# Norm roots moved to ScalarE, and a block of eight modulation units moved from TensorE to GpSimd, in a four-layer float32 transformer kernel

## The chip, the cores and the metric

The kernel runs on one core of a Trainium2 chip. The metric is the device time of one execution in microseconds (us); three executions of the kernel before took 2784.01, 2784.29 and 2785.72 us, median 2784.29.

## The reference

The program computes four transformer layers over 256 tokens of width 1024 in float32. The change touches the first layer's modulation and the norms.

```python
def rms_norm(x, gain=None):
    y = xf * lax.rsqrt(jnp.mean(xf * xf, axis=-1, keepdims=True) + EPS)
...
def _layer_norm(x, g, b):
    mu = jnp.mean(xf, -1, keepdims=True)
    var = jnp.mean(jnp.square(xf - mu), -1, keepdims=True)
    return ((xf - mu) * lax.rsqrt(var + LN_EPS) * g + b)
...
    c_act = jax.nn.silu(c)
    for l in range(DEPTH):
        mod = (c_act @ ada_w[l] + ada_b[l])[:, None, :]
        sh_m, sc_m, gt_m, sh_f, sc_f, gt_f = jnp.split(mod, 6, axis=-1)
        h = rms_norm(x, norm_mix[l]) * (1 + sc_m) + sh_m
        y = hybrid_mixer(h, ...) if l % 2 == 0 else retention_mixer(h, ...)
        x = x + gt_m * y
        h = rms_norm(x, norm_ffn[l]) * (1 + sc_f) + sh_f
        x = x + gt_f * swiglu(h, ffn_w_in[l], ffn_w_out[l])
```

The hybrid mixer has two halves: a gated delta rule (GDN) and a stick-breaking attention (stick). Two more layers follow, each with a mixer of a recurrence and attention, a layer norm (`l1`), a router over 128 groups of experts, and a second layer norm (`l2`).

## The kernel before, in words

**Weights.** All weights come as units of 128x1024 words through a ring of four buffers (`raws`, `NRAW = 4`), loaded by SyncE in the order of the list `units`. The load of unit j waits until unit j-4 has been used up. A unit for an ordinary product is halved: ScalarE rounds it to its high part (`wr<-raw`, 128x1024) and VectorE subtracts that for the low part (`wr<-raw,wr`); TensorE then makes three products of high and low parts. `split()` on both engines does this up to two units ahead of the unit that TensorE is at. A modulation unit (`modulate`, blocks of 512 columns of `ada_w`, four units each) isn't halved: TensorE multiplies it as it is with `cact`, four matmul records of 512 columns per unit. Blocks 7 and 9 (`ADDED`) are already summed by VectorE (`keep<-raw,small,keep`), and one product with a matrix of ones (`add_up`) adds them over the partitions.

**Order.** `order(s)` is one hand-written list of steps which each engine's program runs through. `bg.run(n)` weaves in n steps of background strands (the convolution, `gdn`, `stick`). In the first layer: the first modulation blocks (`FIRST`), twelve `qkv` units, four `gate_rows` units, then the `gdn` strand is added, then the eight units of `SECOND` (blocks 4 and 5) with 3 background steps between, then twelve `stick_rows` units with 3 background steps each (the `stick` strand joins after the eighth), then the sixteen units of `THIRD` with `add_up` of blocks 7 and 9, and the output product `hybrid_out`. The `gdn` strand begins with ScalarE's squares, four sums and their roots (`G.act root`), one chain of small VectorE instructions (`softplus`), transposes (`tok`), and then seven `levels` for two halves of the tokens.

**Norms.** `ada_norm` (before the two feed-forward products and the retention mixer) and `layer_norm` (`l1`, `l2`) have the same shape: squares or statistics for each half a of the tokens, a root per token, a diagonal matrix of the inverse roots (`mod_diag`, `ln_diag`), and TensorE's products with that diagonal, which transpose and scale at once. Before the change VectorE makes the variance (L2487 or L2287), ScalarE the square root, VectorE the reciprocal (L2492) and the diagonal (L2286). `norm_bias` halves the row of biases that TensorE adds with 16 matmuls (`sel,keep_r`).

```python
        def row_scale(tag, v, diag, a):
            dve.wait_ge(*N.act[tag, "root", a])
            dve.reciprocal(v, v).then_inc(*N.dve.up())
            own(N)
            ts(diag[a], ident, v, None, ALU.mult).then_inc(*N.dve.up((tag, "diag", a)))
```

**GpSimd** issues the small loads at the start and the later modulation loads (`aux`); its only arithmetic is in the later mixers (`kin`, L3476).

## Time and profile before

| | |
|---|---|
| median of three executions | 2784.29 us |
| the profiled execution | 2786.23 us |
| its span (first to last instruction) | 2784.4 us |
| TensorE busy | 2720.1 us (98%) |
| VectorE / ScalarE / GpSimd busy | 2206.1 (79%) / 1609.3 (58%) / 87.2 us (3%) |
| mean DMA rate | 208 GB/s |
| granted TensorE clock | 1.0 in the stretches read below |

The profile gives busy time per engine; a busy share near 100% on TensorE says that most of the time is product work, but not that each removed product shortens the run. For that the stretch around it is read: which engine's instruction did the next one wait for. In the lists of rows, PE is TensorE, PEld its weight loads, DVE is VectorE, ACT is ScalarE, POOL is GpSimd and SP is SyncE.

### The profile page before, as it was taken

Reading aid. Unit: us, or ns where it says so; the run is one execution under the profiler, and the core shown is the slowest. Engines: PE = TensorE matmul, PEld = TensorE weight load, DVE = VectorE, ACT = ScalarE, POOL = GpSimd, SP = SyncE. Lnnn points to the kernel's source line nnn. Section 1 sums busy time; section 2 is a strip of 40 time slices with the busy share of each in tenths; the row PEclk is TensorE's granted clock in tenths of the full one; section 3 lists DMA queues with packets and bytes.
Section 4 is the critical chain, followed back from the end, with each engine's and each line's share of the span. In section 5 each row is a group of like instructions: output and inputs, shape, how many; then the busy total and the mean of one; then the engine's idle time right before and its main releaser. Section 6 shows DMA issues by size and latency. Waiting matters only on the chain.

```text
span 2784.4 us, 45458 instructions
## 1 busy us (share of the span) xinstructions
PE 2720.1 (98%) x17102; PEld 2429.6 (87%) x17102; DVE 2206.1 (79%) x3874; ACT 1609.3 (58%) x2793; POOL 87.2 (3%) x154
## 2 busy tenths in 40 slices
PE   8998999999999999999999999999999999999998
PEld 5777888978888989999998888898999999988886
DVE  4766888886665678999887888876799988788887
ACT  3433654345554744778985555555457799754543
POOL 1000101010002000000000000020000000000000
PEclk9999999999999999999999999999999999999999
DMA  8433777764556335666558777762466665687774
GB/s 298 153 114 135 279 257 252 260 247 154 197 189 240 105 136 190 222 212 211 195 196 273 241 242 243 231 213 84 154 209 221 206 208 195 213 269 242 242 242 161
DMA packets 211289, 579.71 MB, mean 208 GB/s; under 512 B 24096, under 2 KB 87872, under 8 KB 210048
## 3 DMA queue, kind: packets, MB, share of 16 engines
q1 hardware_dynamic: 161568, 491.00, 53.2%
q0 software_dynamic: 13792, 53.28, 5.5%
q10 hardware_dynamic: 35712, 32.52, 3.4%
q8 instruction: 138, 2.26, 0.3%
q14 instruction: 79, 0.65, 0.1%
HBM read 541.05 MB, written 35.65 MB: 207 GB/s over the span
## 4 chain that ended last, share of the span: by engine, by line
PE 85%; DVE 9%; ACT 3%; issue 1%; DMA 1%; ACTq 0%; DVEq 0%; POOLq 0%
PE psum L779 84%; DVE gmem L2290 3%; DVE wr L2290 2%; ACT gmem L1636 1%; DVE gmem L2293 1%; ACT wr L1636 1%; DVE xmem L2293 1%; ACT crf L1636 1%; DMA raw<-in_hyb_qkv 0%; DVE wr L2293 0%; DVE small L3125 0%; DVE gmem L2286 0%; DVE gmem L3247 0%; DVE xmem L2290 0%; PE psum L894 0%
## 5 line engine op out<-in xcount | busy, mean ns | idle before, releaser
L779 PE MATMUL psum<-xr,wr 128*128 128x256 f32 (+1 forms) x9776 | 1284.7, 292 | 3.7 <-DVE wr L2290 3.7
L2290 DVE TENSOR_TENSOR wr<-raw,wr 128x1024 fp32r<-128x1024 f32 (+1 forms) x814 | 992.6, 1222 | 365.7 <-ACT wr L1636 361.1
L779 PEld LDWEIGHTS psum<-xr,wr 128*128 128x128 f32 x9776 | 1232.3, 192 | 38.5 <-issue 4.1
L1636 ACT ACTIVATE wr<-raw 128x1024 fp32r<-128x1024 f32 x808 | 845.2, 1050 | 220.9 <-PE psum L779 160.0
L779 PE MATMUL psum<-wr,cr 128*128 128x512 f32 x2064 | 483.0, 389 | 1.8 <-ACT cr L1636 1.8
L779 PEld LDWEIGHTS psum<-wr,cr 128*128 128x128 f32 x2064 | 387.5, 188 | 82.3 <-ACT cr L1636 2.2
L1636 ACT ACTIVATE gmem<-psum 128x512 f32<-128x512 f32 (+2 forms) x303 | 168.9, 570 | 200.4 <-PE psum L779 185.6
L779 PE MATMUL psum<-wr,keep_r 128*128 128x512 f32 x1008 | 243.3, 390 | 0.5 <-DVE wr L2290 0.5
L779 PE MATMUL psum<-wr,xr 128*128 128x512 f32 (+1 forms) x960 | 229.6, 392 | 4.7 <-DVE wr L2290 2.0
L779 PEld LDWEIGHTS psum<-wr,keep_r 128*128 128x128 f32 x1008 | 189.2, 188 | 40.4 <-DVE wr L2290 1.3
L2293 DVE SCALAR_TENSOR_TENSOR oh_r<-cst,keep,keep_r 128x256 fp32r<-128x256 f32 x512 | 213.2, 479 | 0.0
L779 PEld LDWEIGHTS psum<-wr,xr 128*128 128x128 f32 x960 | 172.4, 189 | 45.0 <-issue 6.5
L779 PE MATMUL psum<-gmem 128*128 128x128 f32 (+6 forms) x1320 | 188.5, 295 | 14.8 <-DVE gmem L2290 5.4
L779 PEld LDWEIGHTS psum<-gmem 128*128 128x128 f32 (+1 forms) x1320 | 169.4, 192 | 33.0 <-DVE gmem L2290 7.4
L1636 ACT ACTIVATE cr<-xmem 128x256 fp32r<-128x256 f32 x172 | 72.0, 418 | 215.3 <-PE psum L779 211.1
L1636 ACT ACTIVATE xmem<-psum 128x256 f32<-128x256 f32 x256 | 97.1, 379 | 163.2 <-PE psum L779 153.3
L2290 DVE TENSOR_TENSOR xmem<-xmem,gmem 128x256 f32<-128x256 f32 (+1 forms) x272 | 169.7, 625 | 0.6
L1636 ACT ACTIVATE crf<-cst,keep 128x128 f32<-128x128 f32 x512 | 162.7, 393 | 0.4
L2290 DVE TENSOR_TENSOR gmem<-gmem,psum 128x512 f32<-128x512 f32 x163 | 110.3, 682 | 40.4 <-PE psum L779 25.2
L779 PE MATMUL psum<-wr,hid_r 128*128 128x512 f32 x528 | 122.6, 393 | 0.0
L2290 DVE TENSOR_TENSOR gmem<-gmem 128x256 f32<-128x256 f32 (+10 forms) x195 | 114.0, 593 | 8.8 <-ACT gmem L1636 5.9
L779 PEld LDWEIGHTS psum<-wr,hid_r 128*128 128x128 f32 x528 | 98.9, 188 | 22.5 <-issue 1.9
(193 smaller groups left out, 1732.4 us busy)
## 6 DMA issues: line engine op xcount, KB each, us to landing
raw<-in_uv SPq DMA_DIRECT2D x512, 512.0 KB, 4.7
raw<-in_ffn_in SPq DMA_DIRECT2D x88, 512.0 KB, 4.2
gs<-xmem ACTq DMA_DIRECT2D x248, 128.0 KB, 3.7
xmem<-gs SPq DMA_DIRECT2D x248, 128.0 KB, 4.3
gmem<-in_ada_w POOLq DMA_DIRECT2D x56, 512.0 KB, 4.9
raw<-in_ffn_out SPq DMA_DIRECT2D x44, 512.0 KB, 4.1
raw<-in_ada_w SPq DMA_DIRECT2D x40, 512.0 KB, 4.3
raw<-in_ret_a SPq DMA_DIRECT2D x32, 512.0 KB, 4.3
```

What stands on the lines that cost most here:

```text
L779: ins = pe.matmul(o, a, b, start=first and i == 0, stop=final and i == len(pairs) - 1, skip_group_check=skip)
L1636: return act.activation(o, a, func, **k)
L2290: return dve.tensor_tensor(o, a, b, op)
L2293: return dve.scalar_tensor_tensor(out=o, in0=a, scalar=s, in1=b, op0=op0, op1=op1)
```

## The change

It does five things.

1. `SECOND` is no block of its own: its eight units stand in `units` between the first eight `stick_rows` units, one after each, and `stick_rows` has 5 background steps in place of 3.
2. TensorE no longer multiplies these units. GpSimd scales each half of a unit by its column of `cact` in place and adds it to a sum (`ada_acc`), 30 instructions of 128x512 words in all; a wait on its own semaphore stands between them. SyncE's load of four units later waits for GpSimd (`summed`). TensorE adds each of the two sums up with `add_up`, after the first and third unit of `THIRD`.
3. In `ada_norm` and `layer_norm` the variance, root, inverse and diagonal are made by ScalarE: a logarithm with scale and bias, an exponential with scale -0.5, and the identity scaled by it. VectorE's `row_var` and `row_scale` are gone. The preloaded table is the one with logarithm and exponential.
4. The norm `on` of the attention half (`nsa_turn`) takes the same inverse root.
5. `norm_bias` of `l1` moves from `mix_out` to `mix_col` 11, and the last norm's VectorE steps are reordered.

```diff
+    POOLED = (4, 5)
...
-    add_plain(SECOND)
-    units += [(dr["hyb_a"][c][i], UNIT) for c in range(1, 4) for i in range(4)]
+    pool_unit = {}
+    for r_ in range(12):
+        units.append((dr["hyb_a"][1 + r_ // 4][r_ % 4], UNIT))
+        if r_ < len(SECOND):
+            pool_unit[SECOND[r_]] = len(units)
+            add_plain(SECOND[r_:r_ + 1])
...
-        for i, (m, q) in enumerate(SECOND):
-            if i > 1:
-                bg.run(3)
-            s["modulate"](m, q)
...
                 s["stick_rows"](c, i)
-                bg.run(3)
+                bg.run(5)
+                if 4 * c + i < len(SECOND):
+                    s["modulate"](*SECOND[4 * c + i])
...
             s["modulate"](m, q)
+            if i in (0, 2):
+                s["add_up"](POOLED[i // 2])
...
+        def row_scale(tag, v, bias, scale, diag, a):
+
+            f(v, v, AF.Ln, scale=scale, bias=bias).then_inc(*N.act.up())
+            act.wait_ge(*N.act.now)
+            f(v, v, AF.Exp, scale=-0.5).then_inc(*N.act.up((tag, "root", a)))
+            if diag:
+                act.wait_ge(*N.act.now)
+                f(diag[a], ident, AF.Identity, scale=v).then_inc(*N.act.up((tag, "diag", a)))
...
                     f(used[:, a, e], x[:, a, e], AF.Square,
                       accum_out=small_v[:, i:i + 1]).then_inc(*N.act.up((tag, "sq", i)))
-                v = small_v[:, 4 + a:5 + a]
-                act.wait_ge(*N.dve[tag, "var", a])
-                f(v, v, AF.Sqrt, bias=epsc).then_inc(*N.act.up((tag, "root", a)))
+                    act.wait_ge(*N.act.now)
+                    if n == 0:
+                        f(part, small_v[:, i:i + 1], AF.Identity, scale=1.0 / D, bias=epsc).then_inc(*N.act.up())
+                row_scale(tag, small_v[:, 2 * a + 1:2 * a + 2], part, 1.0 / D, mod_diag, a)
...
-                act.preload_act_table(AF.Sqrt)
+                act.preload_act_table_set("natural_log_exp_and_others")
...
+            if i == 11:
+                act.wait_ge(ln1_in[l], 32)
+                norm_bias(("l1", l), l1b)
...
-                root(S, ("on", l), rn[:, 2:4])
+                inverse_root(S, ("on", l), rn[:, 2:4])
...
-                f(v, v, AF.Sqrt).then_inc(*N.act.up((tag, "root", a)))
+                row_scale(tag, small_v[:, 25 + 2 * a:26 + 2 * a], lneps, 1.0, ln_diag if split_ else None, a)
...
+        pool.wait_ge(*X.act["cact"])
+        for m, q in SECOND:
+            j, acc = pool_unit[m, q], ada_acc[m]
+            pool.wait_ge(raw_in[j % NRAW], 16 * (j // NRAW + 1))
+            for k in range(2):
+                r, c = raws[j % NRAW][:, k * 512:(k + 1) * 512], cact[:, 2 * q + k:2 * q + k + 1]
+                if q + k == 0:
+                    pool.tensor_scalar(acc, r, c, None, ALU.mult).then_inc(*summed.up())
+                else:
+                    pool.wait_ge(*summed.now)
+                    pool.tensor_scalar(r, r, c, None, ALU.mult).then_inc(*summed.up())
+                    pool.wait_ge(*summed.now)
+                    pool.tensor_tensor(acc, acc, r, ALU.add).then_inc(*summed.up(("used", j) if k else None))
```

TensorE's order where the GDN strand starts, before. Names: `wr,xr` is a halved weight unit, `raw,small` a modulation unit, `gmem,cst_60` the four sums of squares, L1025 the transposes.

```order
L779 MATMUL psum<-wr,xr 128x512 x12
L779 MATMUL psum<-raw,small 128x512 x4
L779 MATMUL psum<-gmem,cst_60 128x512 x2
L779 MATMUL psum<-raw,small 128x512 x2
L779 MATMUL psum<-gmem,cst_60 128x512 x2
L779 MATMUL psum<-gmem,cst_60 128x8 x2
L779 MATMUL psum<-raw,small 128x512 x2
L1025 MATMUL psum<-cst_60,gmem 128x128 x12
```

The same place now:

```order
L785 MATMUL psum<-wr,xr 128x512 x24
L785 MATMUL psum<-gmem,cst_60 128x512 x4
L785 MATMUL psum<-wr,xr 128x512 x12
L785 MATMUL psum<-gmem,cst_60 128x8 x2
L1031 MATMUL psum<-cst_60,gmem 128x128 x16
```

The modulation products are gone, and one stick unit stands before the four sums (the other 12 of the first row belong to the last gate unit) and one behind them. The transposes follow the second with no weight unit between them.

ScalarE's order at the same place, before: the gate's activation, the convolution's activation, the table for the sigmoid, the sigmoid, the next table, the squares of the GDN strand.

```order
L1636 ACTIVATE gmem<-psum 128x512 x2
L1636 ACTIVATE gmem<-gmem 128x1024
L1636 ACT_TABLE_LOAD
L1636 ACTIVATE gmem<-gmem 128x8
L1768 ACT_TABLE_LOAD
L1636 ACTIVATE gmem<-gmem 128x512 x4
```

And now:

```order
L1642 ACTIVATE gmem<-psum 128x512 x2
L1642 ACTIVATE gmem<-gmem 128x1024
L1642 ACTIVATE wr<-raw 128x1024
L1642 ACT_TABLE_LOAD
L1642 ACTIVATE gmem<-gmem 128x8
L1785 ACT_TABLE_LOAD
```

The high part of a stick unit now stands ahead of the sigmoid and of the squares.

ScalarE's order at the end of a later mixer, from the norm `on` (128x2) to the norm `l1` (128x1), before:

```order
L1636 ACT_TABLE_LOAD
L1636 ACTIVATE small<-small 128x2
L1636 ACTIVATE wr<-raw 128x1024
L1636 ACTIVATE keep_r<-oh 128x1024
L1636 ACTIVATE small<-small 128x1 x2
L1636 ACTIVATE xr<-psum 128x4x128 x4
```

And now:

```order
L1642 ACT_TABLE_LOAD
L1642 ACTIVATE small<-small 128x2
L1642 ACT_TABLE_LOAD
L1642 ACTIVATE small<-small 128x2
L1642 ACTIVATE wr<-raw 128x1024
L1642 ACT_TABLE_LOAD
L1642 ACTIVATE small<-small 128x1
L1642 ACT_TABLE_LOAD
L1642 ACTIVATE small<-small 128x1
L1642 ACTIVATE gmem<-cst_60,small 128x128
L1642 ACT_TABLE_LOAD
L1642 ACTIVATE small<-small 128x1
```

One more table load, the exponential and the diagonal of the second half follow: six table loads here in place of one, in each of the two later mixers. In the other norms the number of table loads is unchanged. The halving of the bias row (`keep_r<-oh`) has left this place.

## Rows read from the trace of the kernel before

**Rows 1.** The page: the chain that ended last, by engine.
```profile
PE 85%; DVE 9%; ACT 3%; issue 1%; DMA 1%; ACTq 0%; DVEq 0%; POOLq 0%
```

**Rows 2.** Busy time by stretch: the columns are named in the first line.
```profile
core 0: us, PE busy (x) PEld busy (x) DVE busy (x) ACT busy (x) POOL busy (x), PEclk, DMA share, GB/s
89.00:112.00 23.00, 20.55 (x85) 11.98 (x83) 12.84 (x40) 12.67 (x24) 0.00 (x0) 1.00 0.33 110
127.20:163.40 36.20, 35.38 (x210) 30.57 (x208) 25.09 (x33) 12.46 (x15) 0.00 (x0) 1.00 0.46 163
```

**Rows 3.** Timeline, TensorE: start, duration, engine, instruction, [idle before it <- releaser].
```profile
94.59 3.01 PE L779 MATMUL psum<-wr,xr 128*128 128x512 f32 x12
98.29 3.70 PE L779 MATMUL psum<-raw,small 128*128 128x512 f32 x8 [0.69 <-ACT gmem L1636]
103.27 1.96 PE L779 MATMUL psum<-gmem,cst 128*128 128x512 f32 x4 [1.29 <-ACT gmem L1636]
105.07 1.88 PE L779 MATMUL psum<-raw,small 128*128 128x512 f32 x4
106.78 2.22 PE L779 MATMUL psum<-gmem,cst 128*128 128x512 f32 x8
```

**Rows 4.** Timeline, ScalarE, the start of the GDN strand.
```profile
102.50 2.19 ACT L1636 ACTIVATE gmem<-gmem 128x512 f32<-128x512 f32 x4
...
128.66 1.06 ACT L1636 ACTIVATE wr<-raw 128x1024 fp32r<-128x1024 f32 x1 [2.78 <-DMA raw<-in_hyb_a]
```

**Rows 5.** Timeline, GpSimd, first and second later mixer; VectorE beside the second.
```profile
878.82 0.55 POOL L3458 MEMSET gmem<- 128x512 f32 x1
...
882.50 6.29 POOL L3476 TENSOR_TENSOR gmem<-gmem,cols 64x240 f32<-64x240 f32 x8 [0.80 <-ACT gmem L1636]
...
1839.50 1.60 POOL L3476 TENSOR_TENSOR gmem<-gmem,cols 64x240 f32<-64x240 f32 x1
1838.76 1.75 DVE L2290 TENSOR_TENSOR wr<-raw,wr 128x1024 fp32r<-128x1024 f32 x1
```

**Rows 6.** Timeline, all engines, the norm before the first feed-forward product.
```profile
276.32 0.16 DVE L2492 RECIPROCAL small<-small 128x1 f32<-128x1 f32 x1
...
277.53 2.00 PE L779 MATMUL psum<-gmem 128*128 128x128 f32 x16
...
278.69 0.19 ACT L1636 ACTIVATION_READ_ACCUMULATOR gmem<-xmem 128x1 f32 x1
...
280.03 2.05 PE L779 MATMUL psum<-gmem 128*128 128x128 f32 x16 [0.49 <-DVE gmem L2286]
```

**Rows 7.** Timeline, all engines, the norms on and l1 of the first later mixer.
```profile
992.45 1.28 ACT L1636 ACT_TABLE_LOAD   x1
...
993.07 0.16 DVE L2287 TENSOR_SCALAR small<-small 128x2 f32<-128x2 f32 x1
...
997.61 1.22 DVE L2290 TENSOR_TENSOR keep_r<-oh,keep_r 64x1024 fp32r<-64x1024 f32 x1 [3.46 <-ACT keep_r L1636]
998.87 1.23 DVE L2290 TENSOR_TENSOR wr<-raw,wr 128x1024 fp32r<-128x1024 f32 x1
1000.01 0.74 DVE L2293 SCALAR_TENSOR_TENSOR gmem<-psum,small,gmem 128x512 f32<-128x512 f32 x1
...
1007.81 0.21 DVE L3127 BATCH_NORM_AGGREGATE small<-small 128x2 f32<-128x12 f32 x1
...
1009.32 2.05 PE L779 MATMUL psum<-gmem,xmem 128*128 128x128 f32 x16 [1.50 <-DVE gmem L2286]
```

**Rows 8.** Timeline, ScalarE, where the bias halving moves to.
```profile
934.37 0.42 ACT L1636 ACTIVATE gmem<-gmem 128x240 f32<-128x240 f32 x1 [3.25 <-DVE gmem L2290]
```

**Rows 9.** Timeline, the norms l2: aggregate and weight load; the last norm's reciprocal.
```profile
1822.28 0.21 DVE L3127 BATCH_NORM_AGGREGATE small<-small 128x2 f32<-128x12 f32 x1
...
1823.78 1.86 PEld L779 LDWEIGHTS psum<-gmem,xmem 128*128 128x128 f32 x16 [0.32 <-DVE gmem L2286]
...
2778.96 0.16 DVE L3106 RECIPROCAL small<-small 128x1 f32<-128x1 f32 x1
```

More of the change, by code:

```diff
@@ L276, in program @@
     ADDED = (7, 9)
-    added = set()
+    POOLED = (4, 5)
+    added, pooled_units = set(), set()
     def add_plain(blocks):
         for m, q in blocks:
-            (added if m in ADDED else plain).add(len(units))
+            (added if m in ADDED else pooled_units if m in POOLED else plain).add(len(units))
             units.append((dr["ada_w"][0, m, q], UNIT))
@@ L321, in parts_of @@
         return scaled.get(j, [(0, units[j][1], None)])
-    halved = [j for j in range(NU) if j not in plain | added]
+    halved = [j for j in range(NU) if j not in plain | added | pooled_units]
     place_of = {j: k for k, j in enumerate(halved)}
@@ L344, in to_split @@
                 self.next += 1
-                if self.next - 1 not in plain | added:
+                if self.next - 1 not in plain | added | pooled_units:
                     yield self.next - 1
@@ L366, in program @@
     col_in, x_in = sem("col_in"), sem("x_in")
+    summed = Signal(sem("summed"))
     mod_in, nm1_in, ret_in = sem("mod_in"), sem("nm1_in"), sem("ret_in")
@@ L387, in program @@
     gabT = M.get(256)[0:8]
-    ada_acc = {m: keepm[:, 512 * i:512 * i + 512] for i, m in enumerate(ADDED)}
+    ada_acc = {m: keepm[:, 512 * i:512 * i + 512] for ms in (ADDED, POOLED) for i, m in enumerate(ms)}
     m1 = M.mark()
@@ L753, in mod_bank @@
     def mod_bank(m):
-        return FIRST.index((m, 0)) // 4 % 2 if m < 4 else m % 2
+        return FIRST.index((m, 0)) // 4 % 2 if m < 4 else m % 2 if m not in POOLED else 1
     MODS = [(0, 10), (0, 11)] + [(1, m) for m in range(12)]
@@ L919, in add_up @@
             claim(b)
-            pe.wait_ge(*X.dve["acc", m])
+            pe.wait_ge(*(summed["acc", m] if m in POOLED else X.dve["acc", m]))
             mm(bank(b), [(ones, ada_acc[m])]).then_inc(*X.pe.up(("added", m)))
@@ L1714, in ada_norm @@
             for a in range(2):
+                part = small_v[:, 4 + a:5 + a]
                 for n in range(2):
@@ L2431, in modulate @@
                     if q + k == 0:
+                        dve.wait_ge(*X.pe["added", POOLED[ADDED.index(m)]])
                         ts(acc, r, c, None, ALU.mult).then_inc(*X.dve.up())
@@ L2437, in modulate @@
                     X.dve.mark(("acc", m))
-            elif q == 3:
+            elif q == 3 and m not in POOLED:
                 d = mod_dst(m)
@@ L2481, in first_norm @@
                 lo_of("hyb", xr, a, g, 4 + 2 * a + g)
-        def row_var(tag, a):
-            ss = small_v[:, 2 * a:2 * a + 2]
-            dve.wait_ge(*N.act[tag, "sq", 2 * a + 1])
-            dve.tensor_scalar(small_v[:, 4 + a:5 + a], ss[:, 0:1], ss[:, 1:2], 1.0 / D, ALU.add, ALU.mult).then_inc(*N.dve.up((tag, "var", a)))
-        def row_scale(tag, v, diag, a):
-            dve.wait_ge(*N.act[tag, "root", a])
-            dve.reciprocal(v, v).then_inc(*N.dve.up())
-            own(N)
-            ts(diag[a], ident, v, None, ALU.mult).then_inc(*N.dve.up((tag, "diag", a)))
         def ada_norm(tag):
-            row_var(tag, 1)
-            row_scale(tag, small_v[:, 5:6], mod_diag, 1)
             norm_lo(tag)
@@ L2739, in residual @@
                             dve.wait_ge(*A.act["row", 7])
+                        if tag == "ret" and i == 3:
+                            dve.wait_ge(*N.act["ret", "sq", 1])
                         own(X)
@@ L3072, in nsa_turn @@
                 dve.wait_ge(*S.act["ss", l, 0])
-                root(S, ("on", l), rn[:, 2:4], 1.0 / 512, LN_EPS)
+                inverse_root(S, ("on", l), rn[:, 2:4], 1.0 / 512, LN_EPS)
         def mix_half(l):
@@ L3093, in layer_norm @@
             if tag[0] == "l1":
-                dve.wait_ge(*S.dve[("on", tag[1]), "rstd"])
+                dve.wait_ge(*S.act[("on", tag[1]), "root"])
             def center(a, h):
@@ L3098, in center @@
                     ALU.mult).then_inc(*N.dve.up((tag, "h", a, h)))
-            def scale(a):
-                v = mv[:, 2 * a + 1:2 * a + 2]
-                if split_:
-                    row_scale(tag, v, ln_diag, a)
-                else:
-                    dve.wait_ge(*N.act[tag, "root", a])
-                    dve.reciprocal(v, v).then_inc(*N.dve.up())
             def finish(a, h):
                 e = slice(512 * h, 512 * h + 512)
+                dve.wait_ge(*N.act[tag, "root", a])
                 own(N)
@@ L3364, in load @@
                 k = j - NRAW
-                sp.wait_ge(*(X.dve["used", k] if k in added else (W.pe if k in plain else W.dve)[k]))
+                sp.wait_ge(*(X.dve["used", k] if k in added else summed["used", k] if k in pooled_units else (W.pe if k in plain else W.dve)[k]))
             src, n = units[j]
@@ L3418, in pool_program @@
         load(nf0, row("nf0"), rows_in)
+        pool.wait_ge(*X.act["cact"])
[11 more added lines that the diff above has]
+                    pool.tensor_tensor(acc, acc, r, ALU.add).then_inc(*summed.up(("used", j) if k else None))
+            if q == 3:
+                summed.mark(("acc", m))
         def aux(part):
@@ L3499, in program @@
         run(Quiet())
-    for s in [zeroed, kin_made] + [e for t in trios for e in (t.pe, t.act, t.dve)]:
+    for s in [zeroed, kin_made, summed] + [e for t in trios for e in (t.pe, t.act, t.dve)]:
         s.value, s.known = 0, True
```

43 lines of the change are left out of this document (16 added, 27 removed).

## The prediction

> **What bounds the kernel now.** The page comes first: TensorE is busy 98% of the span (the table above) and holds 85% of the chain that ended last [rows 1]. So an edit pays only where it takes work from TensorE or shortens a wait of TensorE. Then the busy times by stretch: from 127.2 to 163.4 us TensorE is busy 35.38 of 36.20 us, while VectorE is busy 25.09; from 89 to 112 us, where the GDN strand starts, TensorE is busy 20.55 and VectorE 12.84 of 23.00 us [rows 2]. The reader is to see that the first-layer stage is TensorE's in its later part, and that at the start of the strand TensorE waits for ScalarE, 0.69 and 1.29 us [rows 3]. Last the timeline around each norm: in every one TensorE waits for a diagonal that VectorE writes, 0.49 us before a feed-forward product, 1.50 us in l1 [rows 6, 7].
>
> A measurement of this kernel can tell about 0.2%, 5.6 us, from no change.
>
> **Term 1, the eight modulation units.** The unit at 105.07 us holds TensorE until 106.78, 1.71 us for four records [rows 3]. Eight of them: 13.7 us taken out. The two new sums over the partitions have two records each, so half a unit, 0.86 us by the same stride: 1.7 us put in. Net -12.0.
>
> **Term 2, cover that is lost.** These units filled waits. Now one stick unit (12 records) stands before the four sums of squares, and ScalarE makes the high part of the next stick unit, 1.06 us [rows 4], before it makes the squares, which started at 102.50 us and will start at about 103.5. The first is finished 0.6 us later. TensorE ends its stick unit at about 100.5 us (the gate's last 12 records start at 94.59 and last 3.01 [rows 3], and the next 12 as long) and waits until 104.1: 3.6 to 3.8 us, in place of 0.69 + 1.29 = 2.0 [rows 3]. +1.8. The roots come 1.06 us later too, so the transposes wait 0.7 us; the first level, whose mask follows a chain of VectorE instructions that had three modulation units beside it, waits some 1.4 us, in place of 0.8. +1.3. Up to here the stage gains 12.0 - 3.1 = 8.9 us. This is an estimate from the order of the instructions and their durations before; between none and 12.0 it lies nearer to the gain because the eight rows of 12 records that follow are all still there as cover.
>
> **Term 3, GpSimd beside VectorE.** No row shows GpSimd's scaling of 128x512 words. Its nearest rows: an addition of 64x240 takes 0.80 us from start to start when alone (eight in 6.29 us), and a memset of 128x512 takes 0.55 [rows 5]. The same addition took 1.60 us at 1839.50, and VectorE's subtraction beside it at 1838.76 took 1.75 instead of 1.23 [rows 5, 7]. So the two engines exclude one another there: each instruction of one held the other up, and the addition held VectorE for 1.75 - 1.23 = 0.52 us per 240 words. For 512 words that makes 1.11 us. For a scaling with one input I take 0.83, the middle of the memset's 0.55 and 1.11; the ends stay in the range. The sum has 30 instructions: 14 additions and 16 scalings, 28.8 us of holding in all, some 40 us of GpSimd's own time with 0.28 us between them (0.80 - 0.52).
>
> When do they run? The first unit can land at about 90 us (its buffer is freed by the halving of the second gate unit near 86, and a load takes 4 to 5 us), in the middle of the convolution on VectorE. Up to the transposes at 112 us GpSimd gets through four units: 8 scalings and 7 additions, 14.4 us of holding. In that stretch VectorE is busy 12.84 of 23.00 us [rows 2], and one more subtraction of 1.22 lies in it now: 61%. The holding that meets a busy VectorE is 14.4 x 0.61 = 8.8 us, and here VectorE is on the path: convolution, squares, the chain of small instructions, the roots, the transposes follow one from the other. I take all 8.8 as delay; the ends are 0 and 14.4. Behind the transposes 14.4 us of holding remain, and VectorE has 11 us of 36 free under a TensorE that is busy [rows 2]: 0, with that free time as its cover, and if it is gone the price is the slower rival's.
>
> The Trainium skill ("SBUF — State Buffer", Who interferes with whom) says that a VectorE instruction with two SBUF inputs and a GpSimd instruction that reads SBUF exclude each other for the whole instruction, whichever is first, and that an instruction with at most one SBUF input is untouched outside the two-port modes. It speaks against this change; the rows of 1838 us agree with its first half, and by its second half the levels, whose subtractions read PSUM, would be held up less than the convolution.
>
> GpSimd's pace: 5 us per unit alone, up to 8.5 if each of four instructions waits 0.88 us (1.60 - 0.72) for a subtraction. A stick row with five background steps lasts about 6.2 us (50 us for eight). GpSimd starts 7 us ahead, and a buffer ring of four lets it lag; a wait for a load appears only above 8 us per unit. Price 0. SyncE's queue: a load waits for GpSimd's unit two pairs back, same cover. The later GpSimd loads (`aux`) were issued at 278 us, long after. VectorE's new wait for `added` in `THIRD` and TensorE's for `summed` come after the last unit by 20 us or more: 0.
>
> **Term 4, the three `ada_norm`.** From VectorE's row of residual sums go the reciprocal (0.16, [rows 6]), the diagonal and the variance of the first half, 0.5 us with their gaps. From the last accumulator read, which ends at 278.88, to TensorE's 280.03 there are 1.15 us of four small instructions on two engines [rows 6]; logarithm, exponential and diagonal on one engine should take 0.95. Together 0.7 us each, and TensorE's products for the first half, which last 2.00 from 277.53 [rows 6], end near 279.4, so no more than that. -2.1.
>
> **Term 5, `l1` in two mixers.** The bias row's low part (1.22 at 997.61) and its high part stand between the weights' halving and the first residual sum at 1000.01 [rows 7]; they move away. The subtraction of 998.87 can then run at 996.7 and the sum at 997.9, 2.1 us earlier, if TensorE's half is ready by then (I count on it: the sum at 1000.01 has no wait before it). Reciprocal, diagonal and variance leave VectorE, 0.6 us with gaps. The aggregate of the second half moves from 1007.81 to 1005.2. From its end to TensorE at 1009.32 were 1.30 us [rows 7]; now a logarithm (0.2), a table load (1.28), an exponential (0.2), the diagonal (0.37) and their gaps, 2.25. 2.6 + 1.3 - 2.25 = 1.7 us each, -3.4. Of the six loads only this one is on the path: the load at 992.45 began 0.8 us before the value that its root waited for was written at 993.23 [rows 7], so a load ahead of a logarithm runs inside the wait; those of the norm `on` have 2 us of waiting.
>
> The Trainium skill ("ScalarE: Activation LUTs", What ACT_TABLE_LOAD costs) gives 2.66 us per switch of tables with its drain; by it each load on the path would cost 1.38 us more, and the sum would be 2.8 us smaller; the load of 992.45 was followed by its root 1.29 us after its start, so the row decides.
>
> **Term 6, `l2`.** In the first one, VectorE is freed of 0.4 us and the waits shorten from 1823.78 to the end of the first half's products [rows 9]: -0.5. In the last one reciprocal and variance go: -0.3.
>
> **Term 7, the moved bias halving**, 1.04 us on ScalarE and 1.22 on VectorE in each mixer: 0, under ScalarE's wait of 3.25 us before 934.37 [rows 8]; 2.3 us per mixer if that cover is gone.
>
> **Sum.** -12.0 + 3.1 + 8.8 - 2.1 - 3.4 - 0.8 = -6.4 us. The profiled execution took 2786.2 us, which gives 2779.8; it lies 1.9 us above the median of 2784.3, so the prediction for the median is **2777.9 us**. In words: the norms give 6.3 us, and the moved block gives about nothing, because GpSimd's hold on VectorE eats its 8.9 us.
>
> **Rivals.** (a) *No hold-up on the path*: the contention is real but falls in VectorE's waits for ScalarE. For: VectorE is idle for 44% of the stretch, and small instructions may slip between. Against: the convolution has no gaps. Then -8.9 - 6.3 = -15.2: 2769.1 us. (b) *Table loads uncovered*: if all of the four loads around `l1` stand on the path and not one, 3 x 1.28 x 2 = 7.7 us come back; -6.4 + 7.7 = +1.3: 2785.6 us, no measurable change. For: there are ten more loads in the program. Against: the load at 992.45, inside a wait. (c) *Slower: VectorE becomes the bound of the stage.* Place: the GDN strand from the convolution to the levels. All 28.8 us of holding end on the path, since masks and subtractions are in one chain with TensorE's products: -8.9 + 28.8 - 6.3 = +13.6: 2797.9 us. It decides once more than 15.2 of the 28.8 us are on the path, about half. For: VectorE has to do the halvings of two rows per level too. Against: after 127 us it was free for 11 of 36 us. (d) The change doing nothing of what it says: the orders show that the instructions moved, so this has no chance of its own; in part it is (b).
>
> **How the numbers follow.** Forecast 48%, (a) 22%, (b) 17%, (c) 13%. The forecast's own range is 2771.5 to 2783.5 (term 3's ends of 0 to 14.4 taken by half, the scaling between 0.55 and 1.11). The whole range reaches from (a) with a little more, 2768.0, to (b), 2786.5, and leaves (c) out. Faster by over 0.2% means below 2778.7: six in ten of the forecast, all of (a), a little of (b) and (c): 0.55. Within: the rest of the forecast and most of (b): 0.32. Slower: most of (c), a little of (b): 0.13.
>
> **What would show it.** Right: VectorE's convolution instructions (128x256) of 0.48 us becoming 1.2 to 1.6 us between 90 and 103; the four sums starting after 107 us; GpSimd's additions at 1.3 to 2.3 us; TensorE idle for 8 us or more between 97 and 125; the reciprocal's place at 276.32 reached by the same residual sums within 2 us of that; `l1`'s diagonal products 1.7 us sooner after the last attention product, with one table load between aggregate and diagonal. Wrong: subtractions at 1.23 us beside GpSimd (then (a)); two loads between aggregate and diagonal (then (b)); TensorE waiting for VectorE in the levels, or SyncE for GpSimd (then (c)).

## The result and the profile after

The changed kernel takes 2797.3 us, median of six executions (2793.5 to 2802.6). The kernel before took 2783.1 in the same measurement. The ratio is 1.0052, with a 95% interval of 1.0042 to 1.0062: slower by about 14 us, outside the forecast's range and on its wrong side. A second measurement gave 1.0055 (1.0042 to 1.0068).

The profiled execution took 2798.4 us with a span of 2796.6. Busy time by engine and the chain by engine, from its page:

```profile
PE 2721.2 (97%) x17074; PEld 2432.5 (87%) x17074; DVE 2211.9 (79%) x3833; ACT 1631.9 (58%) x2837; POOL 136.1 (5%) x184
...
PE 85%; DVE 9%; ACT 3%; DMA 1%; issue 1%; POOL 0%; ACTq 0%; DVEq 0%; POOLq 0%
```

The chain reads as before [rows 1]. TensorE has 28 records fewer, the 12.0 us of products, and yet is busy for 2721.2 us where it was busy for 2720.1. Something made its other instructions longer. The busy times by stretch show what; first the changed kernel, then the one before.

```profile
core 0: us, PE busy (x) PEld busy (x) DVE busy (x) ACT busy (x) POOL busy (x), PEclk, DMA share, GB/s
100.00:120.00 20.00, 15.70 (x50) 10.37 (x51) 16.44 (x29) 12.57 (x24) 10.96 (x8) 0.74 0.34 108
...
160.00:180.00 20.00, 14.72 (x72) 12.19 (x71) 10.81 (x13) 5.53 (x10) 0.00 (x0) 0.83 0.25 79
...
200.00:220.00 20.00, 16.08 (x82) 10.59 (x79) 9.60 (x16) 7.36 (x10) 0.00 (x0) 0.91 0.38 128
220.00:240.00 20.00, 17.47 (x114) 15.01 (x115) 11.60 (x19) 3.02 (x5) 0.00 (x0) 0.91 0.42 138
240.00:260.00 20.00, 15.50 (x83) 12.60 (x82) 10.66 (x15) 4.50 (x6) 0.00 (x0) 0.83 0.51 178
```

```profile
100.00:120.00 20.00, 17.99 (x77) 10.26 (x76) 9.99 (x30) 12.12 (x23) 0.00 (x0) 1.00 0.39 132
...
160.00:180.00 20.00, 16.90 (x97) 13.99 (x96) 12.11 (x15) 9.05 (x14) 0.00 (x0) 1.00 0.23 80
...
240.00:260.00 20.00, 17.74 (x107) 15.41 (x108) 9.90 (x13) 6.42 (x10) 0.00 (x0) 1.00 0.42 145
```

The column PEclk is the granted TensorE clock. Before, it is at its full level (2.4 GHz) through the whole stage. Afterwards it falls to the lower level (1.2 GHz) for some microseconds in each of these five rows, which shows as a mean of 0.74 to 0.91 over 20 us. The changed kernel's TensorE timeline says what stands ahead:

```profile
102.61 6.71 PE L785 MATMUL psum<-gmem,cst 128*128 128x512 f32 x8 [3.84 <-ACT gmem L1642]
...
167.34 3.93 PE L900 MATMUL psum<-cst,gmem 128*128 128x128 f32 x16 [5.26 <-DVE gmem L2307]
...
199.71 0.93 PE L785 MATMUL psum<-gmem 64*128 64x256 f32 x8 [1.63 <-DVE gmem L2303]
200.57 3.50 PE L785 MATMUL psum<-raw,small 128*128 128x512 f32 x4
...
209.20 2.02 PE L785 MATMUL psum<-gmem 128*128 128x256 f32 x12 [3.20 <-DVE gmem L2307]
...
221.83 3.45 PE L785 MATMUL psum<-gmem 128*128 128x256 f32 x12 [2.54 <-DVE gmem L2307]
...
252.99 6.65 PE L785 MATMUL psum<-gmem 128*128 128x128 f32 x32 [4.50 <-DVE gmem L2307]
...
262.73 3.01 PE L785 MATMUL psum<-wr,xr 128*128 128x512 f32 x12 [1.35 <-DVE gmem L2307]
```

Four of the low stretches begin with a long wait of TensorE: 3.84, 5.26, 2.54 and 4.50 us. The 32 records at 252.99 last 6.65 us; 32 of the kind last 4.02 before, at the full clock. The length of the wait alone doesn't decide, though: behind 3.20 us at 209.20 the twelve records last 2.02, which is the full clock, and the four records at 200.57, behind waits of no more than 1.8 us, last 3.50 in place of 1.88. The last line is the start of the hybrid output product, at 240.62 us before and at 262.73 now. The Trainium skill ("TensorE: Matmul & The Clock Gate", What's actually happening) says that the array runs at half its clock by default, that activity lifts this, and that an idle engine falls back. The trace agrees with it in kind, and the forecast had no term for it.

For the whole stage, from 75 us to the bias products of the first feed-forward norm, three sums were taken from stretches of 5 us: TensorE's idle time, the full-speed time that the low clock takes at most (5 us times one minus PEclk, added up), and the place where the stage ends.

| kernel | bias products at | TensorE idle | taken by the low clock |
|---|---|---|---|
| before | 275.8 us | 18.3 us | 0.0 us |
| after | 290.8 | 34.3 | 15.3 |
| after, second profile | 288.4 | 33.9 | 11.9 |

The three profiles don't enter the stage at the same moment: the last gate unit starts at 94.59, 91.47 and 92.64 us. From it to the bias products are 181.2, 199.3 and 195.8 us. One profile of this stage can thus differ from the next of the same kernel by 3.5 us.

From there on the two kernels keep pace: the first feed-forward product starts at 281.97 and 296.33 us, 14.4 us apart, and the last expert product at 2773.02 and 2785.17, 12.2 apart. So the norms gave back some 2 us, and all of the loss is in the hybrid stage.

### The profile page after: what moved, and what is told of

Read it like the earlier page. It is cut to its first block, busy times and chain, and to the rows that moved or that the text cites. A ratio compares the mean times of both kernels' runs of the same rounds, so it can differ in the third digit from the quotient of the medians.

```text
span 2796.6 us, 45451 instructions
## 1 busy us (share of the span) xinstructions
PE 2721.2 (97%) x17074; PEld 2432.5 (87%) x17074; DVE 2211.9 (79%) x3833; ACT 1631.9 (58%) x2837; POOL 136.1 (5%) x184
## 4 chain that ended last, share of the span: by engine, by line
PE 85%; DVE 9%; ACT 3%; DMA 1%; issue 1%; POOL 0%; ACTq 0%; DVEq 0%; POOLq 0%
PE psum L785 84%; DVE gmem L2307 3%; DVE wr L2307 2%; DVE gmem L2310 1%; ACT gmem L1642 1%; ACT wr L1642 1%; ACT crf L1642 1%; DMA raw<-in_hyb_qkv 0%; PE psum L900 0%; DVE xmem L2310 0%; DVE wr L2310 0%; POOL gmem L3482 0%; DVE gmem L3237 0%; DMA raw<-in_ret_qk 0%; DVE gmem L2303 0%
```

## Experiments

Each kernel was timed beside the kernel before; differences are between the medians of one measurement.

### The two halves of the change

`e_norms` is the kernel before with items 3 to 5 alone. `e_pool` has items 1 and 2 alone.

> The kernel before with the norm parts of the change alone (roots, scales and diagonals on ScalarE, the halved bias moved), the second modulation block back on TensorE ahead of the stick rows. Both theories put the loss in the hybrid stage and expect the norms to gain what the intervals in the two traces differ by: ffn0 0.60, ret 0.77, ffn1 0.74, first l1 0.85, second l1 with the mixer ahead of it 2.9, less about 1.5 that one mixer lost to a low granted clock: 2783.1 - 4 to 6 = 2777 to 2780. If instead the norms are part of the loss, 2783 or more.

> The kernel before with the second modulation block's part of the change alone (eight units on GpSimd between the stick rows), norms as before. Both theories: all of the loss is here, 14.4 us later at the first feed-forward product plus the 0.6 that the first norm gave back: 2783.1 + 15 = 2798, between 2794 and 2802. If the two parts disturb each other, it is under 2790.

`e_norms` took 2780.5 us against 2783.7, ratio 0.9990 (0.9981 to 0.9999). `e_pool` took 2800.7, ratio 1.0071 (1.0056 to 1.0086). -3.2 and +17.0 give +13.8, the whole change, so no disturbance between the halves shows. The norms gained slightly less than expected.

### GpSimd's work cut, order and loads kept

```diff
-                    pool.tensor_scalar(r, r, c, None, ALU.mult)
+                    pool.tensor_scalar(r[:, 0:1], r[:, 0:1], c, None, ALU.mult)
...
-                    pool.tensor_tensor(acc, acc, r, ALU.add)
+                    pool.tensor_tensor(acc[:, 0:1], acc[:, 0:1], r[:, 0:1], ALU.add)
```

> The changed kernel with 29 of GpSimd's 30 instructions... all but the two that start a sum, cut to one column of 512 (the second block's two sums are then wrong): order, loads and waits stay, the holding goes. Theory C (lost cover: TensorE has nothing to do between the stick rows, waits longer, and its granted clock falls to the lower level behind each long wait): most of the loss stays, 2790 or more. Theory G (GpSimd holds VectorE up, and so the chain that TensorE waits for): the loss goes, 2783 or less.

2789.7 us, +6.0 (ratio 1.0021, 1.0011 to 1.0032), between the two theories and nearer to C. Of the 14 us, 8 are GpSimd's work. The other 6, and the 3 that the norms win, are lost without it. The timelines show how the 8 come about. First GpSimd and VectorE in the changed kernel, columns as in [rows 3]:

```profile
98.59 1.56 POOL L3420 TENSOR_SCALAR raw<-raw,small 128x512 f32<-128x512 f32 x1 [0.17 <-POOL keep L3422]
100.24 1.26 POOL L3422 TENSOR_TENSOR keep<-keep,raw 128x512 f32<-128x512 f32 x1
101.59 2.48 POOL L3420 TENSOR_SCALAR raw<-raw,small 128x512 f32<-128x512 f32 x1
104.15 1.26 POOL L3422 TENSOR_TENSOR keep<-keep,raw 128x512 f32<-128x512 f32 x1
...
100.28 2.45 DVE L2307 TENSOR_TENSOR gmem<-gmem 128x8 f32<-128x8 f32 x3
...
104.25 1.19 DVE L2303 TENSOR_SCALAR small<-small 128x8 f32<-128x8 f32 x1 [1.04 <-ACT small L1642]
```

The timeline of the same VectorE instructions beside the quiet GpSimd:

```profile
100.04 1.36 DVE L2307 TENSOR_TENSOR gmem<-gmem 128x8 f32<-128x8 f32 x3
...
104.11 0.17 DVE L2303 TENSOR_SCALAR small<-small 128x8 f32<-128x8 f32 x1 [2.50 <-ACT small L1642]
```

An instruction of eight columns took 1.19 us in place of 0.17. It began 0.10 us after GpSimd's addition and ended 0.03 us after it: it was held for the whole of it. It reads a single operand from SBUF.

Where the delay arises shows in TensorE's timelines, counted from the last gate unit (91.47 us in the changed kernel, 92.84 in the quiet one). The changed kernel is 1.5 us later at the four sums (102.61 and 102.47), 2.7 at the second transposes (115.18 and 113.90), 4.5 at the next waiting product (132.58 and 129.43) and 5.6 at the stick transposes (167.34 and 163.09). The second profile has 1.4, 2.6, 4.4 and 5.5. More than half of it arises behind the transposes.

### The products alone taken out

`e_cut` is `e_norms` in its old order, with the products of the second block over 8 columns in place of 512. GpSimd does nothing in it.

> The kernel before with the norms alone (2780.5), old order, with the eight units' products of the second block cut from 512 columns to 8 (its two sums are then wrong); GpSimd does nothing, loads and steps are unmoved. The forecast's first term (TensorE bound): about 12 us go, 2768. Theory L (the strands' round trips over ScalarE and VectorE set the stage, the products only fill their waits): nothing goes, 2779 to 2782, TensorE idles 12 us more. Theory L with K: the new idle stretches bring the low clock, 2782 to 2790, slower though there is less work.

2779.8 us, -3.6 (ratio 0.9984, 0.9975 to 0.9993); `e_norms` had -3.2 (0.9990). This is the central run: some 10.6 us of products (two units 3.70 - 1.06 us, four times) leave TensorE in the old order, and next to nothing is gained. TensorE's timeline in it, to be held against [rows 3]:

```profile
97.54 1.06 PE L780 MATMUL psum<-raw,small 128*128 128x8 f32 x8 [0.69 <-ACT gmem L1638]
102.53 3.75 PE L780 MATMUL psum<-gmem,cst 128*128 128x512 f32 x4 [3.93 <-ACT gmem L1638]
...
125.66 3.00 PE L780 MATMUL psum<-wr,xr 128*128 128x512 f32 x12 [1.87 <-DVE wr L2303]
```

The two units ahead of the four sums shrank from 3.70 to 1.06 us, and the wait behind them grew from 1.29 to 3.93. The four sums then run at the low clock, 3.75 us for what took 1.96. The first stick row starts at 125.66, where `e_norms` has it at 125.58, and the bias products at 274.4, where `e_norms` has them at 274.3. TensorE was busy for 17.99 of 20 us here, but taking work from it won nothing: ahead of the four sums it waits for ScalarE and at the first stick row for VectorE, and the products had filled such waits.

The waits are half of the story. Over the stage TensorE idles 23.7 us in `e_cut` and 18.4 in `e_norms`, 5.3 more, and the low clock takes 5.1 where it took 0.0; together nearly the 10.6 us. What this kernel would take if the clock had stayed up was not run, so how much of the missing gain is the strands' pace and how much the clock stays open.

### TensorE's products kept, in the new places

`e_pe_between` has the order of the changed kernel, with the units multiplied by TensorE; `e_pe_ahead` puts each unit ahead of the five strand steps.

> The changed kernel with GpSimd's work taken back by TensorE: the eight units keep their new places between the stick rows and the strand steps their new count, but each unit is multiplied there by TensorE, in banks 1 and 3, and GpSimd does nothing. Theory C: TensorE has 8 x 1.7 us more of its own work in the gaps, the clock stays up, and the time is near that of the kernel before with the new norms, 2775 to 2784. Theory G expects no more than with the quiet GpSimd: the same time as that run plus up to 13.7 us of products where they don't fall into gaps.

> The kernel with the eight units multiplied by TensorE between the stick rows (2801.7), each unit now ahead of the five strand steps instead of behind them. Theory W (cover counts only where it stands ahead of the step that waits): the waits of 3.90 and 4.15 us shrink by about 1.7 each, and with them the low clock behind: 2788 to 2797. If the place doesn't matter: 2801.

2801.7 (+18.0) and 2794.5 us (+8.7). The first is far from theory C (2775 to 2784) and inside theory G's bound (2789.7 and up to 13.7 more). With nothing on GpSimd, and with all of TensorE's products back, it is no faster than the changed kernel. The place of the cover is worth 9 us: behind the steps that wait it is only added work. Beside `e_quiet`, which has this order without the eight units' products, `e_pe_between` is 12.0 us slower and `e_pe_ahead` 2.8. So the same products that `e_cut` shows to be free in the old order cost 12.0 of their 13.7 us in this one, behind the steps. The wait ahead of the four sums fell from 3.90 to 2.18 us, as expected; the one ahead of the stick transposes was 5.25 and 4.15 before the move, not shorter, since no unit stands between the ninth row and them.

### Fewer steps between the rows

> The changed kernel with four strand steps behind each stick row instead of five. Theory W (five steps bring TensorE to the strands' products before ScalarE and VectorE have their inputs ready, 5.26 us at the stick transposes above all): fewer steps per row let the stick row that stands ahead cover the wait; 2797.3 becomes 2788 to 2794. Against it: the steps left over stand between the later products, where TensorE has 1.9 us units to cover them; then 2797 or more.

> The changed kernel with three strand steps behind each stick row, as in the kernel before: 24 steps of the 60 go to the third block's stretch. Theory W: the transposes' wait falls to the 1.1 us of before and the low clock behind it goes: 2785 to 2792. Against it: what is left of the strands is then run through at the end without cover: 2797 or more.

Four steps took 2809.0 us (+26.1), three 2797.6 (+14.7). Theory W failed; the case against it came, 2797 or more. With three steps the hybrid output product starts at 241.44 us, as early as before, but then TensorE waits at the strand's end, 4.38 us ahead of the last turn, and the bias products stand at 292.0. The waits moved on. Why four are worse than both three and five was not found; its stage has 30.8 us taken by the low clock, the most of all.

### Throwaway products in the waits

```diff
                 claim(4 + i)
+                if i == 0:
+                    for _ in range(3):
+                        mm(bank(4), [(ones, cst0)])
                 pe.wait_ge(*G.act["sq", i])
```

> The changed kernel with eight throwaway products of 128x128 by 128x512 on TensorE, where it idles: three ahead of the wait for the four sums (3.84 us idle at 102.6), five ahead of the wait for the stick transposes (5.26 us idle at 167.3). They hold about 1.0 us each at the full clock and change no other engine's work. Theory K (the clock is part of the loss: each long idle stretch is followed by TensorE at the lower of its two levels, as the 0.69 and 0.63 at 100 to 110 us and the 0.68 and 0.64 at 165 to 175 us show): the two low stretches go, each worth about 3.4 us, 2797.3 becomes 2790 to 2794. Theory N (the low stretches cost nothing, since VectorE's chain sets the stage): 2797 or a little more.

> The changed kernel with 17 throwaway products of about 1.0 us each on TensorE, the eight of the run before and nine more: three and two ahead of the third and fourth exponent sums of the stick part (3.20 and 2.54 us idle), four ahead of the first product with the inverse (4.50 us idle). Theory K (low clock behind idle stretches is the loss): the low stretches at 200, 220 and 250 us go too, and 2797.3 becomes 2783 to 2790, though TensorE has 17 us more to do. Theory N: 2797 to 2805, since the products are work and VectorE's chain sets the stage.

> The changed kernel once more, so that the runs with throwaway products and moved steps stand beside it on one chip: 2797.3, between 2793 and 2803.

`e_fill` took 2794.5 us (+11.5; its ratio of 1.0051 can't be told from the changed kernel's 1.0052), `e_fill_all` 2793.2 (+7.4), the changed kernel in the latter's company 2799.4 (+13.7). Seventeen products more on TensorE made the kernel 6 us faster, ratio 1.0032 (1.0019 to 1.0044) beside 1.0055. In `e_fill_all` the low clock takes 5.1 us of the stage and not 11.9, and the wait at the third exponent sum, 3.20 us, is mostly gone in TensorE's timeline:

```profile
205.33 2.84 PE L785 MATMUL psum<-cst 128*128 128x512 f32 x6
208.64 2.02 PE L785 MATMUL psum<-gmem 128*128 128x256 f32 x12 [0.47 <-DVE gmem L2321]
```

It is a gain, but less than theory K asked: 2793, not 2783 to 2790. That part of the low clock fell into waits, where it costs nothing, would explain it; no run separates the two.

> The changed kernel with the quiet GpSimd (one column of 512) and the 17 throwaway products together: 2789.7 was the one, 2793.2 the other, 2798 neither. If hold-up and clock are separate shares, they add: 2798 - 8 - 5 = 2785, 2782 to 2787. What is then still above the 2780.5 of the norms alone is the order of the steps, whose 12.0 us of saved products won nothing.

2792.0 us (+8.8): the shares don't add. With GpSimd quiet, the fill brought nothing (2789.7 without it). The low clock takes 6.8 us of this stage, all of it behind one place, 216 to 234 us.

### The price of the clock by itself

The stalls stand in the second products of the first expert layer, where TensorE has no wait.

```diff
+            if l == 0 and e in STALLS:
+                claim(6)
+                for _ in range(5):
+                    mm(bank(6), [(ones, cst0)])
+                pe.wait_ge(*stalled[e])
```

> The fastest kernel so far (the norms alone with the table loaded ahead, 2774.5) with ten stalls in the first expert layer's second products, where TensorE is busy without a gap: there it waits for a chain of 15 one-column GpSimd instructions, started by its own last product, 0.34 us each by the run with the quiet GpSimd, some 5.3 us. Nothing else is changed. Theory K: each stall costs its idle time and 3.4 us more at the lower clock behind it: 2774.5 + 10 x 8.7 = 2861 (2850 to 2870). Theory N: idle time alone, 2774.5 + 53 = 2828.

> The same ten stalls of the same length, with five throwaway products ahead of each wait, so that TensorE is busy for about 5 of the 5.3 us. Both theories: 2774.5 + 53 = 2828 (2820 to 2835), with no low clock. The difference to the run with the bare stalls is the price of the clock alone: K 34 us, N 0.

> Ten stalls of a chain of four such instructions, some 1.8 us each. Theory K by the rows seen so far (idle of 1.3 to 1.8 us alone was not followed by the low clock in the kernel before's stage; 2.4 us in the norms behind the mixers was): 2774.5 + 18 = 2793, with no or few low stretches. If any gap in a busy run of TensorE costs the clock: 2820 or more.

Bare stalls: 2863.2 us. The same with five throwaway products each: 2836.7, just above the expected 2820 to 2835, since GpSimd's chain took 5.8 us and not 5.3. Short ones: 2795.8. One bare stall in the timelines of GpSimd and TensorE:

```profile
1589.69 5.82 POOL L3496 TENSOR_SCALAR small<-cst 128x1 f32<-128x1 f32 x15 [24.78 <-PE psum L782]
...
1595.56 5.49 PE L782 MATMUL psum<-wr,cr 128*128 128x512 f32 x12 [5.96 <-POOL small L3496]
1600.85 3.12 PE L782 MATMUL psum<-wr,keep_r 128*128 128x512 f32 x12
```

TensorE's timeline behind a filled stall:

```profile
1592.58 3.03 PE L782 MATMUL psum<-wr,cr 128*128 128x512 f32 x12 [1.68 <-POOL small L3496]
1595.45 2.88 PE L782 MATMUL psum<-wr,keep_r 128*128 128x512 f32 x12
```

And behind a short one:

```profile
1581.98 3.02 PE L782 MATMUL psum<-wr,cr 128*128 128x512 f32 x12 [1.67 <-POOL small L3496]
```

An idle wait of 5.96 us costs (2863.2 - 2836.7) / 10 = 2.7 us more than one of the same length that is filled up to its last 1.68 us; the next twelve records take 5.49 in place of 3.03. A wait of 1.67 us costs itself, 2.1 us with what lies around it, and no clock. This settles theory K for a place where TensorE is the bound. The expected 3.4 us was the price of a fully busy low stretch; part of it lay in the wait.

### Mends, and a faster kernel

```diff
+            if a == 0:
+                act.preload_act_table_set("natural_log_exp_and_others")
             act.wait_ge(*S.dve["sum", l, a])
```

> The kernel before with the new norms alone (2780.5) and one function table loaded ahead, where ScalarE idles before the last turn of each later mixer, so that the five loads inside the first norms behind the mixers go, two of them (1.28 us each) between VectorE's variance and the second diagonal, where TensorE idles 2.41 us. If those loads are on the path: two layers, 1.3 to 2.4 us each: 2776 to 2778. If TensorE waits for the variance anyway: 2780.5.

> The changed kernel with the function table loaded ahead in the later mixers and nothing else. Worth 6.0 us in the kernel with the norms alone, so 2798 - 6 = 2792 (2788 to 2795); what the mended kernel (2785.5) has less is the later start of the strand steps and of the stick strand, about 6.

> The changed kernel with three mends: the function table loaded ahead in the later mixers (worth 6.0 in the kernel with the norms alone), no strand step behind the first stick row, so that the second stands ahead of the four sums, and the stick strand started one row later, so that the tenth row stands ahead of its transposes. Theory W: the waits of 3.84 and 5.26 us fall to under 1.5, the two low stretches behind them go: 2797.3 - 6.0 - 5 to 9 = 2782 to 2786, still above the 2774.5 without GpSimd. If the waits only move on to the next step: 2791.

The first is 2774.5 us, ratio 0.9970 (0.9958 to 0.9981): 8.5 us faster than the kernel before, and the fastest kernel of the study. That is more than the 2776 to 2778 expected. The timelines of ScalarE and TensorE in the changed kernel, at the second half of the first `l1`:

```profile
1018.08 1.28 ACT L1642 ACT_TABLE_LOAD   x1
1020.28 0.29 ACT L1642 ACTIVATE small<-small 128x1 f32<-128x1 f32 x1 [0.92 <-DVE small L3123]
1020.59 1.28 ACT L1642 ACT_TABLE_LOAD   x1
1021.89 0.20 ACT L1642 ACTIVATE small<-small 128x1 f32<-128x1 f32 x1
1022.12 0.40 ACT L1642 ACTIVATE gmem<-cst,small 128x128 f32<-128x128 f32 x1
...
1022.58 2.97 PE L785 MATMUL psum<-gmem,xmem 128*128 128x128 f32 x16 [2.41 <-ACT gmem L1642]
```

The same place with the table loaded ahead:

```profile
1004.33 0.53 ACT L1637 ACTIVATE small<-small 128x1 f32<-128x1 f32 x2 [3.50 <-DVE small L3119]
1004.89 0.40 ACT L1637 ACTIVATE gmem<-cst,small 128x128 f32<-128x128 f32 x1
...
1005.35 2.05 PE L780 MATMUL psum<-gmem,xmem 128*128 128x128 f32 x16 [1.55 <-ACT gmem L1637]
```

The load between logarithm and exponential was on the path. Without it the wait is 1.55 us and not 2.41, and the products behind it run at the full clock, 2.05 and not 2.97 us. In `e_norms` the wait is 2.41 too; from the mixer's last transposes to the end of `l1`'s products it takes 2.1 us more than the kernel with the table loaded ahead, in each of the two layers. Of these 0.9 are this wait, 0.8 the clock behind it, and 0.4 stand at the first half.

In the changed kernel the same mend gave 2793.6 us (+10.3, ratio 1.0031), within expectation. With no strand step behind the first stick row and the stick strand started one row later as well, `e_tuned` took 2785.5 us against 2785.8 for the kernel before, ratio 1.0004 (0.9995 to 1.0012). The later start is thus worth 7.5 us by the ratios and 10.5 by the medians. The total came as expected, the mechanism did not: in its profile, an execution of 2790.4 us, TensorE still waits 3.31 us at 115.35, 3.57 at 137.73 and 4.33 at the stick transposes (171.39), and the stage has 32.7 us idle and 13.6 taken by the low clock. What won the time is open. GpSimd's version gets back to no change, 8 us behind the norms alone with their table.

## Why the prediction was wrong

The loss is the sum of four differences, each from a pair of runs (each against the kernel before beside it):

| step | from | us, by medians | us, by ratios |
|---|---|---|---|
| the new norms | `e_norms` | -3.2 | -2.8 |
| the products taken out | `e_cut` less `e_norms` | -0.4 | -1.7 |
| the new places of rows, loads and steps | `e_quiet` less `e_cut` | +9.6 | +10.3 |
| GpSimd's work | `e_after_again` less `e_quiet` | +7.7 | +9.5 |

By the intervals of the ratios a row that is a difference of two runs is good to some 4 to 5 us. The split between the second and third row holds for this sequence of steps: had the order been changed first, with the products still on TensorE (`e_pe_between`), it would have cost 21.2 us, and taking the products out would then have won 12.0. Their sum, +9.2 where the forecast had -8.9, doesn't depend on the sequence.

**Term 1 failed, and with it the forecast.** It put -12.0 us for products that are worth about nothing where they stood (-0.4 for 10.6 us of them). The reading behind it was "the first-layer stage is TensorE's in its later part", from a busy share of 35.38 in 36.20 us [rows 2]; but the eight units stood ahead of that part, between 98 and 127 us. A TensorE that is busy with fillers looks the same as one that is the bound. What tells them apart is the other side of the trade: the stage kept its length when the fillers went, 180.6 us from the last gate unit to the bias products in `e_cut` and 181.3 in `e_norms`. Taking 12.0 for certain, with an end of "none" that was named and then dropped, was the choice that cost the most.

**Term 2 was mis-sized.** It priced the lost cover at +3.1 us; the new order costs +9.6, with the low clock in it. Its first line was right in detail: a wait of 3.6 to 3.8 us ahead of the four sums was forecast and 3.84 came. But the waits further on were not looked for (5.26 us ahead of the stick transposes at 167.34, 4.50 at 252.99), and no term stood for the clock behind them. The text spoke of granted clocks nowhere, though the table of the profile before had the level of 1.0 as a condition of every duration.

**Term 3 had the reason and nearly the size right, and the place wrong.** It forecast 8.8 us for GpSimd's hold on VectorE, and the run gives 7.7; held instructions of 1.2 us and more are there. But it put all 8.8 ahead of the transposes and nothing behind them, under VectorE's free time. The profiles show 2.7 us up to the second transposes and 2.9 more up to the stick transposes. That the sum agrees is in part luck. Two of its sizes were off against each other: a scaling takes 1.56 us, more than an addition's 1.26, where 0.83 of holding was taken for one and 1.11 for the other. The first unit started at 86.41 us, 5.06 ahead of the last gate unit; by the clock of the kernel before, whose gate unit starts at 94.59, that is 89.5, and "about 90" was right.

**Term 4 was right:** the three intervals from bias products to the first product behind the norm fell by 0.60, 0.77 and 0.74 us, forecast 0.7 each. **Term 5** was forecast at -1.7 each, and up to the start of the second half's products it holds: counted from the mixer's last transposes (1005.98 and 1957.74 us), they start after 16.60 us in both layers, where it was 18.15 before. That is 1.55 sooner. The aggregate moved by 2.6 us, as forecast. What TensorE made of it depended on the clock: the second half's products went from 2.05 to 2.97 us in the first layer and from 3.79 to 2.46 in the second, so that the two norms gained 0.85 and 2.87 us up to the next product. Of the six loads it saw one on the path, and that was the one that counted most; the run with the table loaded ahead shows 0.4 us per layer more at the first half. **Term 6:** -0.4 in the first `l2`, forecast -0.5; nothing in the last norm, forecast -0.3. Terms 4 to 6 were 6.3 us together and add up to 6.2 in these intervals, yet `e_norms` won only 3.2 in the medians, and its interval ends at 5.3. The intervals hold clock luck of the profiled executions (the 3.79 us above); where the rest went is open.

**The rivals.** Rival (c) gave 2797.9 us and 2797.3 came, but by other means: it had all 28.8 us of holding on the path and term 1's gain with it. Holding cost a quarter of that. The condition that it named (VectorE becomes the bound) was never tested against the chain being the bound already. Rival (b), loads uncovered in `l1`, was not the loss, since the norms won time; but it was nearer than it looked: loading the table ahead won some 5 us more (2774.5 beside 2780.5, 5.3 by the differences), where (b) had 7.7 for all the loads around `l1`.

## What to carry to other kernels

Before pricing work taken from a busy engine, cut that work to a few columns and run it: if the time stays, the work was filler in that place. It says nothing of another place: the same products were free in the old order and cost 12.0 us behind the waiting steps. Where a strand's round trips set a stage, an engine's busy share says nothing of the bound, and the place of a filler counts as much as its length: it has to stand ahead of the step that waits. Look at the granted clock beside every wait of TensorE; a gap of 5.96 us cost itself and 2.7 us more in the next products.

## What the runs showed of the hardware

**The clock costs 2.7 us behind a wait of 5.96 us and nothing behind one of 1.67 us** (the stalls above). In between the length of the wait doesn't settle it. In the changed kernel the low level followed 2.54 us at 221.83 and the 2.41 in `l1`, but not 3.20 at 209.20 nor 1.35 at 262.73. In the quiet kernel it did not follow 2.54 us at 217.46 (2.02 us for the same twelve records). A wait of 2.21 us at the same step was followed by it in `e_cut` (3.39 us for four records of 512 columns) and not in `e_norms` (1.98).

**The clock also fell while TensorE was busy.** In the fastest kernel it did so behind products with a single column. TensorE's timeline there:

```profile
964.43 1.90 PE L780 MATMUL psum<-cst,gmem 128*128 128x1 f32 x16
```

The stretch behind it, columns as in the busy times above:

```profile
965.00:970.00 5.00, 5.00 (x28) 4.77 (x29) 3.75 (x15) 3.13 (x10) 0.00 (x0) 0.66 0.33 105
```

The kernel before has the same sixteen records twice. Behind those at 1917.53 us the clock is 0.66 over five microseconds, behind those at 967.20 it stays up (TensorE's timeline, then the busy times by stretch):

```profile
967.20 1.90 PE L779 MATMUL psum<-cst,gmem 128*128 128x1 f32 x16
...
968.00:973.00 5.00, 5.00 (x34) 4.55 (x35) 3.85 (x15) 3.03 (x10) 0.00 (x0) 1.00 0.30 105
```

So these products alone don't decide it, and what does was not tried.

**GpSimd holds one-operand instructions too.** The Trainium skill ("SBUF — State Buffer", Who interferes with whom), cited in the prediction, has a VectorE instruction with at most one SBUF input untouched unless it enters a two-port mode, and lists `tensor_scalar` among those that can. The trace has an eight-column `TENSOR_SCALAR` from SBUF to SBUF at 1.19 us beside GpSimd and 0.17 without, and one of 128x256 in the convolution at 1.36 (90.75 us) and 0.34. That agrees with the page if the instructions entered such a mode, which no row shows; for planning, they were held.
